# The levels of a block inverse on the half of the columns that each level changes

## The chip, the cores and the metric

The kernel runs on one core of a Trainium2 chip. The metric is the device time of one execution in microseconds (us), the median of several runs. TensorE is PE in the profile (PEld its weight loads), VectorE is DVE, ScalarE is ACT, GpSimd is POOL, SyncE is SP.

## The reference

Two transformer blocks run one after the other on 512 tokens of width 1024. The first has attention with rotary positions beside a convolution branch. The second mixes tokens with a recurrence (RWKV-7) of 12 heads of width 64, beside attention over a memory, and then has a feed-forward layer. All is fp32. The part that this case touches is the recurrence:

```python
def step(S, inp):
    r_t, w_t, k_t, v_t, a_t, b_t = inp
    sa = jnp.einsum('bhvk,bhk->bhv', S, a_t)
    S = (S * w_t[:, :, None, :] + sa[..., None] * b_t[:, :, None, :]
         + v_t[..., None] * k_t[:, :, None, :])
    return S, jnp.einsum('bhvk,bhk->bhv', S, r_t)
```

## The kernel before

The engines run five programs that are written out by hand and wait for one another by semaphores. There is no scheduler: the order of each engine is the order of its code. PSUM has eight banks; `psum_order` lists every product in the order in which PE makes it, with its bank.

The recurrence is done in chunks of C = 64 tokens, for NP = 6 pairs of heads. A pair has 2 heads x 8 chunks = 16 systems of 64 rows. The chunks are split by parity q over the two halves of the 128 partitions, so an operand of one head is `[rows(q), h, c, :]` with c in 0 to 3 and 64 columns. For each system the kernel needs X, the inverse of I - N, with N strictly triangular. X starts as the inverse of the 2x2 diagonal blocks and grows by levels b = 2, 4, 8, 16, 32: a level knows the diagonal blocks of size b and fills in those of size 2b. It keeps X twice, as `XN` and transposed as `XT`, side by side in `XX`. In the level loop of pair p, for both heads h:

- PE, `times_inverse` (L982): y = NT x XN, 8 matmuls for each head, each with a 64x64 stationary operand and 64 moving columns. The result is in PSUM as `y{b}_{p}_{h}`, 256 columns.
- DVE (L2026): Y = y times the mask `m{b}`, which leaves the off-diagonal blocks of the level; 128x256.
- PE, `inverse_update` (L992): two products for each system, Y with XT (L1000) and XT with Y (L1003), 16 matmuls for each head, one PSUM tensor of two banks. In the last level `last_update` (L1008, matmul in L1013) makes the first of the two alone.
- DVE (L2052): the products are added into X, in the half of the columns that the level changes: 128x256 out of both banks, 128x128 in the last level.

Each such fp32 matmul stands in the trace as two records of MATMUL and two of LDWEIGHTS: 8 matmuls for each of two heads are "x32".

Other work is written between these steps. On PE: in level 2 the mean of the group norm of pair p - 1 (`gn_mean`), in level 4 its squares and the value projection of pair p + 1 in two halves, in level 8 `masked_values` (L1026), in level 16 the gate and `bonus_sum`. On DVE: in level 2 `gn_centre` and `unit_key`, in level 4 `decayed_a`, in level 8 the input of the next v, `gn_finish` and a `weights_low` (L1663), in level 16 `decayed_b`, `gate` and `bonus`. In the last pair, p = 5, units of the memory attention (`memory_unit`) stand there. After the levels comes `solve` (L1036), which multiplies by XT with 128 moving columns. L955 are the transposes ahead of the levels, L977 products of keys before these, L714 the modulation products, with a stationary operand of 2 columns, L727 small transposes of 2 moving columns.

POOL does little: it clears `GLU` (L629), waits until the norm of the second block's input is summed, clears the first state `H` (L631), and then makes one product for each pair (L641).

Of the kernel before, what the change touches and what calls it, by code (L numbers as in the profile page):

```python
# [63 lines left out]
G = 4  # L64
# [254 lines left out]
def build(nc, small, tables, xT, ctxT, memT, weights, saved, outT):  # L319
    plan = psum_plan()  # L320
    with ExitStack() as ctx:
# [86 lines left out]
        at = half + 6 * S  # L408
        XX_AT = at
        XX = region(at, 2, S); at += 2 * S  # L410
        NT, Y, TK, TV, MAK, MRK = (region(at + i * S, NC, C) for i in range(6)); at += 6 * S
        GT, RP, FB = (region(at + i * S, NC, C) for i in range(3)); at += 3 * S

        def heads_first(x):
            return x.rearrange("p (h c) t -> p h c t", h=HEADS)
# [5 lines left out]
        NT, Y, MAK, MRK = map(heads_first, (NT, Y, MAK, MRK))  # L421
        TK, TV = map(pairs_first, (TK, TV))

        inputs = 10 * S
# [41 lines left out]

        def rows(half):
            return slice(half * DH, (half + 1) * DH)

        def by_head(name):  # L470

# [59 lines left out]
        def bank_on(name):  # L531

            return psum[:, plan[name][0] * S:8 * S]

        def is_full(name):

# [108 lines left out]
        def _(pe):  # L645
# [345 lines left out]

            def inverse_update(name, h):  # L992

                take(name)
                out = bank(name).rearrange("p (k c t) -> p k c t", k=2, t=C)
# [12 lines left out]
            def last_update(name, h):  # L1008

                out = take(name, G * C).rearrange("p (c t) -> p c t", c=G)  # L1010
                for c in range(G):
                    for q in range(PARITIES):
                        ins = pe.matmul(out[rows(q), c, :], Y[rows(q), h, c, :], XT[rows(q), h, c, :],  # L1013
                                        start=True, stop=True)
                        if c == G - 1:
                            full_inc(ins, name)

# [74 lines left out]
            for p in range(NP):  # L1092
# [14 lines left out]
                for b in LEVELS:  # L1107
                    for h in range(HEADS):
                        if prev is None:
                            pe.wait_ge(x_first, p + 1)  # L1110
                        else:
                            pe.wait_ge(*is_free(f"x{prev}_{p}_{h}"))
                        times_inverse(f"y{b}_{p}_{h}", h)

                    if p and b == LEVELS[0]:
                        gn_mean(p - 1)
# [12 lines left out]
                    for h in range(HEADS):  # L1129

                        pe.wait_ge(*is_free(f"y{b}_{p}_{h}"))
                        if b != LEVELS[-1]:
                            inverse_update(f"x{b}_{p}_{h}", h)
                        else:

                            last_update(f"xf_{p}_{h}", h)
# [442 lines left out]
        def _(vec):  # L1579
# [426 lines left out]
            for p in range(NP):  # L2006
# [15 lines left out]
                for b in LEVELS:  # L2022
                    for h in range(HEADS):
                        name = f"y{b}_{p}_{h}"
                        vec.wait_ge(*is_full(name))
                        free_inc(vec.tensor_tensor(Y[:, h], bank(name, G * C).rearrange("p (c t) -> p c t", c=G),  # L2026
                                                   mask(f"m{b}", G), ALU.mult), name)

                    if p and b == LEVELS[0]:
                        gn_centre(p - 1)  # L2030
# [8 lines left out]
                    for h in range(HEADS):  # L2039

                        if b != LEVELS[-1]:
                            name = f"x{b}_{p}_{h}"
                            vec.wait_ge(*is_full(name))
                            new, old = (y[:, at:at + 2 * (S - b)].rearrange("p (k n) -> p k n", k=2)[:, :, 0:G * C]
                                        .rearrange("p k (n two b) -> p k n two b", two=2, b=b)[:, :, :, 0, :]
                                        for y, at in ((bank_on(name), b), (work, XX_AT + h * G * C + b)))
                        else:
                            name = f"xf_{p}_{h}"
                            vec.wait_ge(*is_full(name))
                            new, old = (y.rearrange("p (n two b) -> p n two b", two=2, b=b)[:, :, 1, :]  # L2050
                                        for y in (bank(name, G * C), XX[:, 0, h * G * C:(h + 1) * G * C]))
# [256 lines left out]
```

## Time and profile before

| | us |
|---|---|
| median of 3 runs | 1251.21 (1249.71 to 1251.71) |
| the profiled execution, device time | 1245.89 |
| its span, first to last instruction | 1243.8 |
| PE busy | 1124.5 (90%) |
| DVE busy | 648.4 (52%) |
| ACT busy | 458.1 (37%) |
| the level stages of pairs 0 to 5 | from about 480 to 805 |

Span and busy times come from one profiled execution. Its device time is 5.3 us below the median of the runs. The busy time of an engine is summed over the span, where the stages have different limits. [...]

### The profile page before, as it was taken

To read this page: it belongs to the slowest core of one execution; us is meant where nothing else is said; L and a number is where in the kernel's file an instruction comes from. 1 tells how busy PE (TensorE), PEld (TensorE's weight loads), DVE (VectorE), ACT (ScalarE), POOL (GpSimd) and SP (SyncE) were. 2 spreads that over 40 slices of the span, in tenths; PEclk is the share of its full clock that TensorE was granted. 3 is DMA by queue.
4 is the path that set the end of the run, shared out by engine and by line. 5 is a ranking of instruction groups with operands and counts; after the bars stand their busy time and mean duration, and the time that the engine had idled before them with its cause. 6 is when DMAs were issued, how large, how long until landed. Compare 5 with 4: busy or idle time off the path is not lost.

```text
span 1243.8 us, 21886 instructions
## 1 busy us (share of the span) xinstructions
PE 1124.5 (90%) x9476; PEld 837.2 (67%) x9476; DVE 648.4 (52%) x1057; ACT 458.1 (37%) x736; POOL 9.9 (1%) x12
## 2 busy tenths in 40 slices
PE   6999999677799787888888898899799999999998
PEld 4377776344468566666666665668588888888887
DVE  2478777886544666464655643674633323233332
ACT  3233353346642453323232322352445311345211
POOL 0000000000000000000000000000000000000000
PEclk9999999799899898989899999999899999999999
DMA  8832223200022211101010003103233333323330
GB/s 320 294 121 66 85 85 114 73 1 1 1 71 82 74 62 38 38 32 36 19 36 19 19 3 121 52 26 101 61 92 94 102 102 88 99 85 102 102 110 26
DMA packets 25582, 94.93 MB, mean 76 GB/s; under 512 B 2833, under 2 KB 2833, under 8 KB 24977
## 3 DMA queue, kind: packets, MB, share of 16 engines
q1 hardware_dynamic: 25488, 93.54, 23.3%
q8 instruction: 76, 1.25, 0.4%
q14 instruction: 18, 0.14, 0.0%
HBM read 89.34 MB, written 4.19 MB: 75 GB/s over the span
## 4 chain that ended last, share of the span: by engine, by line
PE 50%; DVE 9%; ACT 2%; issue 2%; ACTq 0%; DVEq 0%
PE psum L689 13%; PE psum L690 13%; PE psum L691 13%; PE psum L699 3%; PE psum L987 2%; PE psum L1000 1%; PE psum L1036 1%; DVE pair_weights_low L1663 1%; DVE work L2052 1%; PE psum L955 1%; PE psum L1003 1%; PE psum L1079 1%; DVE work L2014 1%; PE psum L1059 1%; PE psum L1013 1%
## 5 line engine op out<-in xcount | busy, mean ns | idle before, releaser
L1663 DVE TENSOR_TENSOR weights_low<-ring,weights_high 128x1024 fp32r<-128x1024 f32 x72 | 88.2, 1225 | 82.8 <-ACT weights_high L1334 82.8
L1334 ACT ACTIVATE weights_high<-ring 128x1024 fp32r<-128x1024 f32 x72 | 75.9, 1054 | 127.7 <-PE psum L691 127.7
L689 PE MATMUL psum<-normed_high,weights_high 128*128 128x512 f32 x256 | 102.7, 401 | 4.8 <-DVE normed_low L1668 4.2
L690 PE MATMUL psum<-normed_low,weights_high 128*128 128x512 f32 x256 | 102.1, 399 | 0.0
L691 PE MATMUL psum<-normed_high,weights_low 128*128 128x512 f32 x256 | 101.9, 398 | 0.0
L689 PE MATMUL psum<-hidden_high,weights_high 128*128 128x512 f32 x256 | 99.6, 389 | 0.0
L690 PE MATMUL psum<-hidden_low,weights_high 128*128 128x512 f32 x256 | 99.6, 389 | 0.0
L691 PE MATMUL psum<-hidden_high,weights_low 128*128 128x512 f32 x256 | 99.6, 389 | 0.0
L1284 ACT ACTIVATE work<-psum 128x384 f32<-128x384 f32 (+2 forms) x124 | 59.6, 510 | 96.1 <-PE psum L1036 51.0
L689 PE MATMUL psum<-pair_normed_high,pair_weights_high 128*128 128x512 f32 x176 | 76.6, 435 | 12.3 <-DVE normed_low L1668 4.3
L2141 DVE TENSOR_TENSOR hidden_low<-work,hidden_high 128x512 fp32r<-128x512 f32 x32 | 22.2, 693 | 110.3 <-ACT hidden_high L1573 110.3
L1592 DVE SCALAR_TENSOR_TENSOR work<-work,small_sb 128x512 f32<-128x512 f32 x116 | 79.2, 745 | 0.0
L689 PE MATMUL psum<-normed_high,in_weights_high 128*128 128x512 f32 x176 | 71.6, 407 | 1.6 <-DVE in_weights_low L1663 1.6
L691 PE MATMUL psum<-pair_normed_high,pair_weights_low 128*128 128x512 f32 x176 | 69.7, 396 | 0.0
L690 PE MATMUL psum<-normed_low,pair_weights_high 128*128 128x512 f32 x176 | 69.7, 396 | 0.0
L691 PE MATMUL psum<-normed_high,in_weights_low 128*128 128x512 f32 x176 | 69.6, 396 | 0.0
L690 PE MATMUL psum<-normed_low,in_weights_high 128*128 128x512 f32 x176 | 69.6, 395 | 0.0
L689 PEld LDWEIGHTS psum<-normed_high,weights_high 128*128 128x128 f32 x256 | 48.5, 189 | 19.4 <-issue 5.4
L691 PEld LDWEIGHTS psum<-normed_high,weights_low 128*128 128x128 f32 x256 | 48.7, 190 | 11.8
L690 PEld LDWEIGHTS psum<-normed_low,weights_high 128*128 128x128 f32 x256 | 48.7, 190 | 11.2
L689 PEld LDWEIGHTS psum<-hidden_high,weights_high 128*128 128x128 f32 x256 | 48.0, 188 | 10.1
L691 PEld LDWEIGHTS psum<-hidden_high,weights_low 128*128 128x128 f32 x256 | 48.0, 188 | 10.0
(235 smaller groups left out, 2115.2 us busy)
## 6 DMA issues: line engine op xcount, KB each, us to landing
ring<-weights SPq DMA_DIRECT2D x154, 512.0 KB, 3.6
residual<-xT SPq DMA_DIRECT2D x1, 2048.0 KB, 18.4
residual_saved<-residual SPq DMA_DIRECT2D x8, 256.0 KB, 2.0
residual<-residual_saved SPq DMA_DIRECT2D x1, 2048.0 KB, 8.7
outT<-residual SPq DMA_DIRECT2D x8, 256.0 KB, 3.2
work<-memT SPq DMA_DIRECT2D x1, 1024.0 KB, 5.0
work<-ctxT SPq DMA_DIRECT2D x1, 1024.0 KB, 9.7
small_sb<-small SPq DMA_DIRECT2D x1, 907.0 KB, 7.7
```

The costliest lines, as they stand in the source:

```text
L689: pe.matmul(out, wh, high(k), start=first and n == 0, stop=False)
L690: pe.matmul(out, wh, low(k), start=False, stop=False)
L691: ins = pe.matmul(out, wl, high(k), start=False, stop=last and n == len(order) - 1)
L699: full_inc(pe.matmul(take(name, w), stationary, moving, start=True, stop=True), name)
L955: last = pe.transpose(out[:, c, :], src[:, 2 * c:2 * c + 2, :], tab("ident"))
L987: ins = pe.matmul(out[rows(q), c, :], NT[rows(1 - q), h, c, :], XN[rows(1 - q), h, c, :], start=True, stop=True)
L1000: ins = pe.matmul(out[rows(q), 0, c, :], Y[rows(q), h, c, :], XT[rows(q), h, c, :], start=True, stop=True)
L1284: free_inc(act.activation(out, bank(name, w) if src is None else src, ACT.Copy), name)
L1334: act.activation(WH[group(q)][:, q % 2, :], ring[:, SLOT[b], :], ACT.Copy).then_inc(w_high, 1)
L1592: return vec.scalar_tensor_tensor(out=out, in0=a, scalar=scalar, in1=b, op0=op, op1=ALU.add)
L1663: vec.tensor_tensor(WL[group(q)][:, q % 2, :], ring[:, SLOT[b], :], WH[group(q)][:, q % 2, :].bitcast(F32), ALU.subtract).then_inc(w_low, 1)
L2141: vec.tensor_tensor(FL[:, t, :], FS[:, t, :], FH[:, t, :].bitcast(F32), ALU.subtract).then_inc(h_low, 1)
```

## The change

A level changes only the columns of its odd blocks of X (in the transposed copy; even blocks in the other), and Y is zero in half of its columns. The change moves only these columns through PE.

- `times_inverse` takes only the even blocks of XN as moving columns, 32 in place of 64, and writes 32 columns for each system. The mask reads 128x128 and writes into the even blocks of Y.
- The odd blocks of Y have to be zero, and the even blocks differ from level to level. So each level has a Y of its own, `Y[b]`, in a region `YS` of 5 x 512 words for each partition. POOL clears it once, after `H`, and the first mask of pair 0 waits for that.
- `inverse_update` and `last_update` take 32 columns in place of 64 as moving operand, out of XT (odd blocks) or Y (even blocks). The whole Y or XT is still the stationary operand, 64x64.
- The additions have the same shape. They now read whole, contiguous PSUM rows instead of every second block.
- The regions that follow NT in the work buffer move by one place.

```diff
+        YS = region(at, len(LEVELS), S)
...
+        def blocks_of(x, b, odd):
+
+            return x.rearrange("p (n two b) -> p n two b", two=2, b=b)[:, :, odd, :]
...
             pool.memset(H[:, 0, :], 0.0).then_inc(zeroed, 1)
+            pool.memset(YS, 0.0).then_inc(zeroed, 1)
...
-            def times_inverse(name, h):
+            HALF = C // 2
...
-                out = take(name, G * C).rearrange("p (c t) -> p c t", c=G)
+            def times_inverse(name, h, b):
+
+                out = take(name, G * HALF).rearrange("p (c t) -> p c t", c=G)
                 for c in range(G):
                     for q in range(PARITIES):
-                        ins = pe.matmul(out[rows(q), c, :], NT[rows(1 - q), h, c, :], XN[rows(1 - q), h, c, :],
-                                        start=True, stop=True)
+                        ins = pe.matmul(out[rows(q), c, :], NT[rows(1 - q), h, c, :],
+                                        blocks_of(XN[rows(1 - q), h, c, :], b, 0), start=True, stop=True)
...
-                                ins = pe.matmul(out[rows(q), 0, c, :], Y[rows(q), h, c, :], XT[rows(q), h, c, :],
-                                                start=True, stop=True)
+                                ins = pe.matmul(out[rows(q), 0, c, :], Y[b][rows(q), h, c, :],
+                                                blocks_of(XT[rows(q), h, c, :], b, 1), start=True, stop=True)
                             else:
-                                ins = pe.matmul(out[rows(1 - q), 1, c, :], XT[rows(q), h, c, :], Y[rows(q), h, c, :],
-                                                start=True, stop=True)
+                                ins = pe.matmul(out[rows(1 - q), 1, c, :], XT[rows(q), h, c, :],
+                                                blocks_of(Y[b][rows(q), h, c, :], b, 0), start=True, stop=True)
...
                         vec.wait_ge(*is_full(name))
-                        free_inc(vec.tensor_tensor(Y[:, h], bank(name, G * C).rearrange("p (c t) -> p c t", c=G),
-                                                   mask(f"m{b}", G), ALU.mult), name)
+                        new = bank(name, G * C // 2).rearrange("p (c n b) -> p c n b", c=G, b=b)
+                        kept = Y[b][:, h].rearrange("p c (n two b) -> p c n two b", two=2, b=b)[:, :, :, 0, :]
+                        m = blocks_of(tab(f"m{b}"), b, 0)[:, None].to_broadcast([P, G, C // (2 * b), b])
+                        if (p, b, h) == (0, LEVELS[0], 0):
+                            vec.wait_ge(zeroed, 3)
+                        free_inc(vec.tensor_tensor(kept, new, m, ALU.mult), name)
...
-                            new, old = (y[:, at:at + 2 * (S - b)].rearrange("p (k n) -> p k n", k=2)[:, :, 0:G * C]
-                                        .rearrange("p k (n two b) -> p k n two b", two=2, b=b)[:, :, :, 0, :]
-                                        for y, at in ((bank_on(name), b), (work, XX_AT + h * G * C + b)))
+                            new = bank(name).rearrange("p (k n) -> p k n", k=2)[:, :, 0:G * C // 2].rearrange(
+                                "p k (n b) -> p k n b", b=b)
+                            at = XX_AT + h * G * C + b
+                            old = work[:, at:at + 2 * (S - b)].rearrange("p (k n) -> p k n", k=2)[:, :, 0:G * C].rearrange(
+                                "p k (n two b) -> p k n two b", two=2, b=b)[:, :, :, 0, :]
```

No instruction changes its place. What PE issues in level 2 of pair 0 was this (times_inverse for both heads, then the first matmuls of inverse_update; the last figures are partitions x moving columns, and a matmul counts once here):

```order
L987 MATMUL psum<-work 64x64 x16
L1000 MATMUL psum<-work 64x64
L1003 MATMUL psum<-work 64x64
L1000 MATMUL psum<-work 64x64
L1003 MATMUL psum<-work 64x64
```

and in the changed kernel it is this:

```order
L992 MATMUL psum<-work 64x32 x16
L1005 MATMUL psum<-work 64x32
L1008 MATMUL psum<-work 64x32
L1005 MATMUL psum<-work 64x32
L1008 MATMUL psum<-work 64x32
```

The number of matmuls and their order stay; only the moving columns are halved. On DVE, levels 16 and 32 of pair 1 were (masks, `decayed_b`, additions, `gate`, `bonus`, masks, last additions):

```order
L2026 TENSOR_TENSOR work<-psum,tables_sb 128x256 x2
L1957 TENSOR_TENSOR work<-work 128x512
L1961 TENSOR_TENSOR work<-work 128x512
L2052 TENSOR_TENSOR work<-psum,work 128x2x8x16 x2
L1978 TENSOR_TENSOR mixed<-psum,mixed 128x512
L1935 TENSOR_TENSOR work<-psum,work 128x512
L2026 TENSOR_TENSOR work<-psum,tables_sb 128x256 x2
L2052 TENSOR_TENSOR work<-psum,work 128x4x32 x2
```

and in the changed kernel they are:

```order
L2036 TENSOR_TENSOR work<-psum,tables_sb 128x8x16 x2
L1962 TENSOR_TENSOR work<-work 128x512
L1966 TENSOR_TENSOR work<-work 128x512
L2063 TENSOR_TENSOR work<-psum,work 128x2x8x16 x2
L1983 TENSOR_TENSOR mixed<-psum,mixed 128x512
L1940 TENSOR_TENSOR work<-psum,work 128x512
L2036 TENSOR_TENSOR work<-psum,tables_sb 128x4x32 x2
L2063 TENSOR_TENSOR work<-psum,work 128x4x32 x2
```

The masks have half of their elements, in runs of b; nothing else differs.

## Rows read from the trace of the kernel before

**Rows 1.** The head of the page.
```profile
span 1243.8 us, 21886 instructions
...
PE 1124.5 (90%) x9476; PEld 837.2 (67%) x9476; DVE 648.4 (52%) x1057; ACT 458.1 (37%) x736; POOL 9.9 (1%) x12
```

**Rows 2.** Windows over the level stages of pairs 1 and 4.
```profile
core 0: us, PE busy (x) PEld busy (x) DVE busy (x) ACT busy (x) POOL busy (x), PEclk, DMA share, GB/s
536.20:560.70 24.50, 21.91 (x515) 16.82 (x516) 14.96 (x31) 4.71 (x8) 0.00 (x0) 1.00 0.08 24
716.30:742.60 26.30, 23.70 (x515) 17.82 (x515) 14.94 (x31) 4.69 (x7) 0.00 (x0) 0.92 0.01 2
```

**Rows 3.** The chain that ended last, pair 1, levels 16 and 32: start, us, what.
```profile
555.09 0.67 DVE work L2026 x2
...
557.00 0.75 DVE work L2052 x2
...
558.94 0.34 DVE work L2026
...
559.32 1.15 PE psum L1013 x32
```

**Rows 4.** Timeline of DVE, pair 2, levels 2, 4 and 8.
```profile
598.83 0.69 DVE L1592 SCALAR_TENSOR_TENSOR mixed<-psum,mixed 128x512 f32<-128x512 f32 x1 [0.59 <-PE psum L699]
...
605.87 0.42 DVE L2052 TENSOR_TENSOR work<-psum,work 128x256 f32<-128x256 f32 x1 [3.49 <-PE psum L1003]
...
611.99 0.89 DVE L2052 TENSOR_TENSOR work<-psum,work 128x256 f32<-128x256 f32 x2 [0.23 <-PE psum L1000]
```

**Rows 5.** Groups by line and form: masks and additions.
```profile
L2026 DVE TENSOR_TENSOR work<-psum,tables_sb 128x256 f32<-128x256 f32 x60 | 23.8, 419 | 11.4 <-PE psum L987 11.1
L2052 DVE TENSOR_TENSOR work<-psum,work 128x256 f32<-128x256 f32 x48 | 19.8, 422 | 37.3 <-PE psum L1003 33.7 <-PE psum L1000 2.7
L2052 DVE TENSOR_TENSOR work<-psum,work 128x128 f32<-128x128 f32 x12 | 3.5, 292 | 3.8 <-PE psum L1013 3.8
```

**Rows 6.** Timeline of PE: runs of records of one line.
```profile
600.13 1.15 PE L987 MATMUL psum<-work 64*64 64x64 f32 x32 [0.25 <-DVE work L2052]
...
621.00 1.96 PE L1036 MATMUL psum<-work 64*64 64x128 f32 x32 [0.16 <-issue]
...
57.60 0.62 PE L727 MATMUL psum<-tables_sb,work 2*128 2x2 f32 x8
```

**Rows 7.** By line: durations in ns, minimum/median/maximum, first and last start.
```profile
L714 PEld LDWEIGHTS psum<-ring,small_temps x48: 80/85/85, 28.1 to 219.8; 128*2 128x2 f32 x48
...
L987 PEld LDWEIGHTS psum<-work x960: 129/135/228, 480.6 to 800.9; 64*64 64x64 f32 x192
L987 PE MATMUL psum<-work x960: 218/218/366, 480.6 to 800.9; 64*64 64x64 f32 x192
...
L699 PEld LDWEIGHTS psum<-head_squares,tables_sb x44: 186/188/338, 25.5 to 828.0; 128*128 128x128 f32 x44
...
L1036 PE MATMUL psum<-work x192: 269/269/321, 501.3 to 807.0; 64*64 64x128 f32 x192
...
L727 PEld LDWEIGHTS psum<-tables_sb,work x8: 133/136/138, 57.6 to 58.0; 2*128 2x128 f32 x8
L727 PE MATMUL psum<-tables_sb,work x8: 190/196/197, 57.6 to 58.0; 2*128 2x2 f32 x8
```

**Rows 8.** Timeline of POOL.
```profile
0.73 1.91 POOL L629 MEMSET work<- 128x2168 f32 x1 [0.29 <-POOLq L2300]
```

**Rows 9.** Windows at the low clock, and the product of keys ahead of pair 3.
```profile
529.30:536.00 6.70, 5.48 (x47) 4.71 (x48) 6.28 (x10) 2.83 (x5) 0.85 (x1) 0.50 0.05 22
590.70:597.40 6.70, 5.38 (x44) 4.65 (x46) 4.71 (x8) 2.39 (x4) 0.00 (x0) 0.50 0.00 0
710.20:720.30 10.10, 8.46 (x66) 5.71 (x62) 6.17 (x10) 2.84 (x5) 0.00 (x0) 0.50 0.01 2
...
649.26 1.98 PE L977 MATMUL psum<-work 64*64 64x128 f32 x32 [2.65 <-DVE head_rstd L1927]
```

More of the change, by code:

```diff
@@ L410, in build @@
         XX = region(at, 2, S); at += 2 * S
-        NT, Y, TK, TV, MAK, MRK = (region(at + i * S, NC, C) for i in range(6)); at += 6 * S
+        NT, TK, TV, MAK, MRK = (region(at + i * S, NC, C) for i in range(5)); at += 5 * S
         GT, RP, FB = (region(at + i * S, NC, C) for i in range(3)); at += 3 * S
+        YS = region(at, len(LEVELS), S)
         def heads_first(x):
@@ L420, in build @@
         XT, XN = (heads_first(XX[:, i, :].rearrange("p (n t) -> p n t", t=C)) for i in range(2))
-        NT, Y, MAK, MRK = map(heads_first, (NT, Y, MAK, MRK))
+        NT, MAK, MRK = map(heads_first, (NT, MAK, MRK))
+        Y = {b: heads_first(YS[:, i, :].rearrange("p (n t) -> p n t", t=C)) for i, b in enumerate(LEVELS)}
         TK, TV = map(pairs_first, (TK, TV))
@@ L529, in bank @@
             return psum[rows, b * S:b * S + (w or n * S)]
-        def bank_on(name):
-            return psum[:, plan[name][0] * S:8 * S]
         def is_full(name):
@@ L980, in key_products, with inverse_update @@
                             full_inc(ins, name)
-            def times_inverse(name, h):
-                out = take(name, G * C).rearrange("p (c t) -> p c t", c=G)
+            HALF = C // 2
+            def times_inverse(name, h, b):
+                out = take(name, G * HALF).rearrange("p (c t) -> p c t", c=G)
                 for c in range(G):
                     for q in range(PARITIES):
-                        ins = pe.matmul(out[rows(q), c, :], NT[rows(1 - q), h, c, :], XN[rows(1 - q), h, c, :],
-                                        start=True, stop=True)
+                        ins = pe.matmul(out[rows(q), c, :], NT[rows(1 - q), h, c, :],
+                                        blocks_of(XN[rows(1 - q), h, c, :], b, 0), start=True, stop=True)
                         if c == G - 1:
                             full_inc(ins, name)
-            def inverse_update(name, h):
+            def inverse_update(name, h, b):
                 take(name)
-                out = bank(name).rearrange("p (k c t) -> p k c t", k=2, t=C)
+                out = bank(name).rearrange("p (k c t) -> p k c t", k=2, t=HALF)
                 for c in range(G):
@@ L999, in inverse_update, with last_update @@
                             if k == 0:
-                                ins = pe.matmul(out[rows(q), 0, c, :], Y[rows(q), h, c, :], XT[rows(q), h, c, :],
-                                                start=True, stop=True)
-                            else:
-                                ins = pe.matmul(out[rows(1 - q), 1, c, :], XT[rows(q), h, c, :], Y[rows(q), h, c, :],
-                                                start=True, stop=True)
+                                ins = pe.matmul(out[rows(q), 0, c, :], Y[b][rows(q), h, c, :],
+                                                blocks_of(XT[rows(q), h, c, :], b, 1), start=True, stop=True)
+                            else:
+                                ins = pe.matmul(out[rows(1 - q), 1, c, :], XT[rows(q), h, c, :],
+                                                blocks_of(Y[b][rows(q), h, c, :], b, 0), start=True, stop=True)
                             if c == G - 1:
                                 full_inc(ins, name)
-            def last_update(name, h):
-                out = take(name, G * C).rearrange("p (c t) -> p c t", c=G)
+            def last_update(name, h, b):
+                out = take(name, G * HALF).rearrange("p (c t) -> p c t", c=G)
                 for c in range(G):
                     for q in range(PARITIES):
-                        ins = pe.matmul(out[rows(q), c, :], Y[rows(q), h, c, :], XT[rows(q), h, c, :],
-                                        start=True, stop=True)
+                        ins = pe.matmul(out[rows(q), c, :], Y[b][rows(q), h, c, :],
+                                        blocks_of(XT[rows(q), h, c, :], b, 1), start=True, stop=True)
                         if c == G - 1:
@@ L1112, in _ @@
                             pe.wait_ge(*is_free(f"x{prev}_{p}_{h}"))
-                        times_inverse(f"y{b}_{p}_{h}", h)
+                        times_inverse(f"y{b}_{p}_{h}", h, b)
                     if p and b == LEVELS[0]:
@@ L1132, in _ @@
                         if b != LEVELS[-1]:
-                            inverse_update(f"x{b}_{p}_{h}", h)
+                            inverse_update(f"x{b}_{p}_{h}", h, b)
                         else:
-                            last_update(f"xf_{p}_{h}", h)
+                            last_update(f"xf_{p}_{h}", h, b)
                         if p + 1 < NP and b == LEVELS[1] and h == 0:
@@ L2049, in _ @@
                             vec.wait_ge(*is_full(name))
-                            new, old = (y.rearrange("p (n two b) -> p n two b", two=2, b=b)[:, :, 1, :]
-                                        for y in (bank(name, G * C), XX[:, 0, h * G * C:(h + 1) * G * C]))
+                            new = bank(name, G * C // 2).rearrange("p (n b) -> p n b", b=b)
+                            old = blocks_of(XX[:, 0, h * G * C:(h + 1) * G * C], b, 1)
                         free_inc(vec.tensor_tensor(old, new, old, ALU.add), name)
```

## The prediction

> **What bounds the kernel now.** The page's head comes first: TensorE (PE) is busy 90% of a 1243.8 us span, and the VectorE (DVE) is busy 52% [rows 1]. That is an average. The change lies in the inversion stage of the six head pairs, so the next view is the table of windows over that stage: 24.5 us for pair 1 and 26.3 for pair 4, with PE busy 21.9 and 23.7 us of it [rows 2]. Outside of the six stages nothing is edited but one memset. PE's busy time counts the whole latency of overlapping small matmuls, so it does not say that PE sets the pace of the stage.
>
> Then the chain of waits, inside one stage (pair 1). From 555.09 us it runs on DVE: both masks of level 16 (0.67), then after `decayed_b` both additions of level 16 (0.75), the first mask of level 32 (0.34), and only then PE's last update [rows 3]. In the earlier levels (timeline of pair 2) it is different. In level 2 the centring of the last pair's output (598.83) stands between the masks and the additions. In level 4 the first addition waits 3.49 us for PE, which has half of the v projection ahead of each update. In level 8 the additions at 611.99 wait 0.23 us for PE [rows 4]. So a shorter mask pays in levels 16 and 32; elsewhere PE or other DVE work sets the time.
>
> **The mask (DVE).** It reads 128x256 out of PSUM in 419 ns; after the change it reads and writes 128x128. The nearest row is the last addition, 128x128 with PSUM in and strided out, 292 ns; the same line at 128x256 takes 422 [rows 5]. It is strided now already, in runs of 2 to 32 elements, and the by-form row gives one mean for all of them, so I price short runs at nothing. A mask saves 419 - 292 = 127 ns. There are 60. On the path:
> - Level 16, pairs 0 to 4: both masks, 2 x 127 = 254 ns, five times: 1.27 us.
> - Level 32, pairs 0 to 4: the first mask only, since the last update then runs through both heads without a gap (1.15 us for both, [rows 3]): 5 x 0.127 = 0.64 us.
> - Level 2 of pair 0, which has no earlier pair to centre: one mask, 0.13 us.
> - Pair 5: PE and the memory attention's units stand between mask and update; nothing.
> Sum 2.04 us. The other 44 masks or so are hidden, by PE's side products and by centring; that is 5.6 us of DVE time with no effect.
>
> **The matmuls (PE).** This is the disputed cost. Each matmul of the three helpers keeps its 64x64 stationary operand and its count, and moves 32 columns in place of 64. A fp32 matmul stands in the trace as two records, each with a weight load. What sets the gap from one record to the next in the same part of the array, the columns that stream or the load?
> - Streaming: with 128 columns (the solve, 32 records in two parts of the array, 1.96 us less its own 0.27 over 15.5 steps) the gap is 109 ns. With 64 columns it is (1.15 - 0.22)/16 = 58, more than the half of 109 [rows 6, 7].
> - Loading: the shortest load, of 2 columns, takes 85 ns, of 64 columns 135, of 128 columns 188 [rows 7]. That is about 50 ns for each 64 columns above a fixed part: a load of 64 columns needs 50 to 53 ns, as long as 64 columns stream.
> - A case where next to nothing streams: the transposes L727 move 2 columns behind a load that lasts 136 ns, as ours does. Eight take 0.62 us; less the 0.196 of the last that is 61 ns a step, not 10 [rows 6, 7].
> So at 32 columns I take the load as the bound and the gap as unchanged at 58. Bounds: from 58 - 27 = 31 ns (streaming alone, half of 53 gone) up to 61 (L727's). What does get shorter is the end of each group: the last record drains 32 columns sooner. 128 columns take 269 and 64 take 218, so 32 save 25 ns [rows 7]. Four or five such ends lie on the chain in each pair (y of level 2, second update of levels 4 and 8, last update): 6 x 4 x 0.025 = 0.6 us.
>
> [...]
>
> **The rest.** The additions keep shape and element count; PSUM is now read contiguously where it was strided: priced at nothing, bound by the 422 against 419 of a contiguous read [rows 5]. Reading the moving operand in runs of 2 or 4 has no row here; if it doubled the stream of 32 columns it would be back at 53 ns, behind the load. The memset of 2560 words a partition runs on POOL after that of `H`, at about 412 us. A memset of 2168 takes 1.91, so this one 2.3, done by 415. The first mask, which waits for it, comes after the first y product at 480.6 [rows 7, 8]. Cover 65 us. If it disturbed DVE, which is then on the path, it would cost at most its own 2.3; no row speaks for it. The separate buffers remove no wait: the masks wait only for their product.
>
> **Sum.** 2.04 + 0.6 = 2.6, so the profiled execution goes from a span of 1243.8 to 1241.2 and from its 1245.9 to 1243.3. The three runs have their median at 1251.2, 5.3 above that execution. 1251.2 - 2.6 = 1248.6.
>
> **The rivals.**
> 1. *The clock, and slower.* Each of pairs 0 to 4 enters the stage out of a stretch at granted clock 0.5 (1.2 GHz), around the place where PE has waited for DVE ahead of its key products (2.65 us in pair 3): 6.7 us before pairs 1 and 2, but 10.1 us around the start of pair 4 [rows 9]. Pair 4's stage takes 26.3 against 24.5 us [rows 2]: a stretch of that extra length costs 1.8 us. The change takes columns away just there, in the first products of the levels. If that lets the low clock last longer, one more such stretch leaves -0.8, two cancel the gain at +1.0, and all four pairs that lack it now give 4 x 1.8 - 2.6 = +4.6, 1255.8. For it: pair 2's low stretch reaches to 597.4, into its y product. Against: before pair 1 it ends before the stage starts at 536.2, and at 0.5 the transposes and products of other lines fill PE as before. It decides from two stretches on.
> 2. *Streaming sets the gap, and much faster.* With 31 in place of 58, a y group of both heads gets 0.43 us shorter, an update of one head 0.21. On the chain of a pair: y of level 2 (0.43), y of level 4 and its two updates (0.6), half of y and the update of level 8 (0.6), the last update (0.2): 1.85 a pair, 11 in six, with the 2.6 above 13.6: 1237.6. For it: the gap does follow columns from 128 to 64. Against: L727 and the load durations. An in-between gap of 45 gives half of the 11, and 1243.1.
> 3. *The masks do not get shorter* (short runs or the repeated mask cost what was saved): only the ends are left, 1250.6, no change. Against: the additions at 292 and 422.
>
> **How the numbers follow.** Load-bound with the clock as now: 0.60. Since its 2.6 us is 0.21% of the time, just at the bound, I give 0.36 of it to faster and 0.24 to same. Rival 2 or the in-between gap: 0.19, all faster. Rival 1: 0.16, half in same (one or two stretches), half slower. Rival 3: 0.05, same. So faster 0.55, same 0.37, slower 0.08. About 0.2% is what a measurement of this kernel tells from no change, which is 2.5 us. The range goes from 1243, the in-between gap, to 1253, two and a half extra stretches; it leaves out the full rival 2 and most of the slower part of rival 1.
>
> **What the profile after will show.** The masks at 128x128 and near 292 ns. If the load sets the gap, 32 records of y still last about 1.13 us, and matmul durations are near 193; if streaming does, they last near 0.7. The stage of pair 1 at 24.0 instead of 24.5. In the windows, the length of each stretch at 0.5: longer than 6.8 in more pairs than one means rival 1. The memset at 412 should last about 2.3 us, and the first mask of pair 0 should have no wait from POOL. I am wrong if the gap falls well under 58, or if the stages get shorter by more than 0.7 us with the masks at 292.

## The result, and the profile after

The changed kernel takes 1273.38 us (median of 4 runs, 1265.43 to 1278.82). The kernel before takes 1251.46 beside it (4 runs, 1249.71 to 1252.88). The ratio is 1.0164, with a 95% interval of 1.0126 to 1.0202: slower. The forecast was 1248.6, with a range up to 1253. A ratio here is not the quotient of the two medians. The ratios further down count every run, except that of the changed kernel with ten idle matmuls, which leaves out the five of its ten runs that lie over 1.5% above the fastest.

The head of the page of the changed kernel, with the granted clock in 40 slices:

```profile
span 1274.2 us, 21888 instructions
...
PE 1156.1 (91%) x9476; PEld 862.0 (68%) x9476; DVE 641.3 (50%) x1057; ACT 458.1 (36%) x736; POOL 12.1 (1%) x13
...
PEclk9999999799999988888887979989899999999999
```

Beside [rows 1], PE has the same 9476 matmuls with fewer columns to move, and yet it is busy for 31.6 us more (1156.1 against 1124.5). DVE is busy 7.1 us less. PE did the same operations on less data and was busy for longer, so it ran slower. The clock row says so (the granted clock is the share of full speed that TensorE was given in a stretch; 1.00 is all of it): of the twelve slices over the levels (the 16th to the 27th) nine show 8 or 7, where the page of the kernel before has three. The mean granted clock of the profiled execution is 0.939; before it was 0.968.

The windows over the six level stages of the changed kernel, each from its first y product to its first product of `solve`:

```profile
core 0: us, PE busy (x) PEld busy (x) DVE busy (x) ACT busy (x) POOL busy (x), PEclk, DMA share, GB/s
480.80:503.40 22.60, 21.67 (x510) 18.39 (x508) 11.37 (x27) 2.75 (x5) 0.00 (x0) 0.85 0.09 26
538.50:567.10 28.60, 26.58 (x514) 20.27 (x514) 13.86 (x31) 4.60 (x7) 0.00 (x0) 0.80 0.08 21
604.20:632.40 28.20, 26.33 (x514) 20.22 (x514) 13.61 (x31) 4.57 (x7) 0.00 (x0) 0.80 0.08 21
668.90:698.40 29.50, 27.13 (x514) 20.81 (x514) 13.58 (x30) 4.56 (x7) 0.00 (x0) 0.79 0.07 20
736.60:765.20 28.60, 26.66 (x514) 20.24 (x514) 13.87 (x31) 4.56 (x7) 0.00 (x0) 0.80 0.01 2
799.40:834.00 34.60, 31.85 (x546) 21.93 (x544) 18.38 (x62) 10.39 (x33) 0.00 (x0) 0.84 0.18 69
sum 172.10, PE 160.22 PEld 121.85 DVE 84.66 ACT 31.42 POOL 0.00; mean PE 26.70 PEld 20.31 DVE 14.11 ACT 5.24 POOL 0.00
```

The sum is 172.1. The same six windows of the kernel before give 20.6, 24.4, 25.1, 24.7, 26.2 and 30.1, together 151.1; [rows 2] has two of them. So the stages have 21.0 of the 30.4 us by which the span grew. Another 7.5 lie between the stages (from `solve` to the next y product: 181.1 against 173.6) and 1.8 after the last one. No stage of the changed kernel has a clock of 1.00; of the kernel before, pair 4 (0.92) and pair 2 (0.97) alone were under it.

The windows over the long stretches at the low clock, a granted clock of 0.50, changed kernel:

```profile
532.80:549.80 17.00, 15.36 (x154) 11.54 (x155) 8.59 (x16) 4.24 (x7) 0.00 (x0) 0.50 0.01 2
597.60:614.70 17.10, 15.77 (x176) 11.72 (x169) 9.46 (x18) 4.79 (x9) 0.15 (x1) 0.50 0.01 2
662.50:679.50 17.00, 15.59 (x171) 11.51 (x164) 9.26 (x17) 4.71 (x8) 0.00 (x0) 0.50 0.01 2
730.70:747.80 17.10, 15.30 (x154) 11.47 (x155) 8.75 (x17) 4.26 (x8) 0.00 (x0) 0.50 0.01 2
822.90:836.60 13.70, 13.70 (x114) 10.29 (x116) 4.18 (x16) 3.12 (x10) 0.00 (x0) 0.51 0.01 1
```

In [rows 9] such a stretch lasted 6.7 us ahead of pairs 1 and 2 and ended about where the levels began; at pair 4 it lasted 10.1. Now it begins near the same place, within about 1 us of the end of PE's wait ahead of the key products, but in pairs 1 to 4 it lasts 17.0 and reaches over level 2 into level 4. Pair 0 has a second stretch of 6.8 us inside its levels, and in pair 5 there is a new one, in the last levels. Added up over the records of the granted clock, the low clock inside the six stages went from 5.6 to 64.6 us. For 59.0 us more of it the stages got 21.0 us longer: 0.36 us for each. PE's busy row doesn't give this away, since 15.36 of 17.00 us is 90% busy. Where the recorded texts write 1.2 and 2.4 GHz, the traces show the shares 0.50 and 1.00; no run shows the frequencies.

The timeline of PE shows where the clock comes back in pair 1:

```profile
543.96 1.92 PE L992 MATMUL psum<-work 64*64 64x32 f32 x32
...
548.53 0.63 PE L694 MATMUL psum<-pair_normed_high,pair_weights_low 128*128 128x512 f32 x1
...
549.99 0.40 PE L692 MATMUL psum<-pair_normed_high,pair_weights_high 128*128 128x512 f32 x1
```

What PE did before it rose was level 2, the y product of level 4, the squares of the group norm and then the v projection, which moves 512 columns with each matmul. Its matmuls came 0.43 us apart at 0.50 and come 0.23 us apart at 1.00. A y product of both heads took 1.92 us at the low clock. At the full clock it takes 1.12, in the same kernel:

```profile
624.18 1.12 PE L992 MATMUL psum<-work 64*64 64x32 f32 x32 [0.26 <-DVE work L2063]
```

The groups by line and form, and the durations by line, of the changed kernel:

```profile
L2036 DVE TENSOR_TENSOR work<-psum,tables_sb 128x128 f32<-128x128 f32 x60 | 16.3, 288 | 18.5 <-PE psum L992 18.4
L2063 DVE TENSOR_TENSOR work<-psum,work 128x256 f32<-128x256 f32 x48 | 19.9, 423 | 50.5 <-PE psum L1008 46.9 <-PE psum L1005 3.2
...
L992 PE MATMUL psum<-work x960: 186/219/313, 480.6 to 826.1; 64*64 64x32 f32 x192
```

The masks take 288 ns, the additions are unchanged [rows 5]. But DVE's waits ahead of the additions grew from 37.3 to 50.5 us, and those ahead of the masks from 11.4 to 18.5. A y record lasts 219 ns at full clock, as long as with 64 columns (218 [rows 7]), and 291 at the low clock; the 186 is a single record.

### The profile page after: what moved, and what is told of

Read it like the earlier page. It is cut to its first block, busy times and chain, and to the rows that moved or that the text cites. A ratio compares the mean times of both kernels' runs of the same rounds, so it can differ in the third digit from the quotient of the medians.

```text
span 1274.2 us, 21888 instructions
## 1 busy us (share of the span) xinstructions
PE 1156.1 (91%) x9476; PEld 862.0 (68%) x9476; DVE 641.3 (50%) x1057; ACT 458.1 (36%) x736; POOL 12.1 (1%) x13
## 4 chain that ended last, share of the span: by engine, by line
PE 52%; DVE 8%; ACT 2%; issue 2%; ACTq 0%
PE psum L692 13%; PE psum L693 12%; PE psum L694 12%; PE psum L702 3%; PE psum L992 2%; PE psum L1041 1%; PE psum L1005 1%; PE psum L958 1%; DVE pair_weights_low L1668 1%; PE psum L1018 1%; PE psum L1084 1%; PE psum L1008 1%; PE psum L910 1%; PE psum L1064 1%; DVE work L2063 1%
## 5 line engine op out<-in xcount | busy, mean ns | idle before, releaser
L692 PE MATMUL psum<-pair_normed_high,pair_weights_high 128*128 128x512 f32 x176 | 80.3, 456 | 12.3 <-DVE normed_low L1673 4.3
L692 PEld LDWEIGHTS psum<-pair_normed_high,pair_weights_high 128*128 128x128 f32 x176 | 34.9, 198 | 31.8 <-issue 11.0
## 6 DMA issues: line engine op xcount, KB each, us to landing
residual<-xT SPq DMA_DIRECT2D x1, 2048.0 KB, 18.5
```

The costliest lines, as they stand in the source:

```text
L692: pe.matmul(out, wh, high(k), start=first and n == 0, stop=False)
```

## The experiments

The theory after the result (theory A in the expectations): with the gap set by the load, PE moves half of the columns in the same time. With that, TensorE is held at a granted clock of 0.50 for longer, into the levels. Its rivals were another cost of the narrow products themselves (operands read in runs of 2 to 32), and a cost of the masks, the separate buffers or the memset. Each expectation stands as it was written ahead of the run. The ratio is always to the kernel before, run on the same chip.

### Masks, buffers and memset alone

All matmuls move 64 columns again. What is left is the short mask, `Y[b]` and the memset. Against the changed kernel:

```diff
-                                        blocks_of(XN[rows(1 - q), h, c, :], b, 0), start=True, stop=True)
+                                        XN[rows(1 - q), h, c, :], start=True, stop=True)
...
-                        new = bank(name, G * C // 2).rearrange("p (c n b) -> p c n b", c=G, b=b)
+                        new = bank(name, G * C).rearrange("p (c n two b) -> p c n two b", c=G, two=2, b=b)[:, :, :, 0, :]
```

and the same in `inverse_update`, `last_update` and the additions.

> Y of each level in its own buffer, cleared once, and masks of 128x128, but every matmul moves all its 64 columns as in the kernel before. Theory A (the time was lost because fewer moving columns keep the clock at 1.2 GHz for longer): the low stretches are those of the kernel before (about 0.967 mean clock, 6.8 us ahead of each pair), and the shorter masks leave their 2 us: 1249.3, ratio 0.998. Theory B (the buffers, the memset or the masks in short runs cost the time): 1265 or more.

Measured: 1247.66 us (12 runs), ratio 0.9977 (0.9951 to 1.0003). None of the loss is in this part. The interval includes 1, so the runs alone don't show the 2 us of the masks. The stretches were not quite those of the kernel before: in the profiled execution those of pairs 1 to 4 last 10.2 us and end inside the stage, as here in pair 2, and of the low clock 16.1 us fall into the stages, where the kernel before has 5.6 and the changed one 64.6:

```profile
596.40:622.20 25.80, 23.53 (x517) 17.69 (x515) 13.86 (x31) 4.39 (x7) 0.00 (x0) 0.93 0.07 23
```

### The y products alone, and the updates alone

Two kernels take the changed one apart by function. The first moves 32 columns in `times_inverse` only (960 of the 2688 records), the second in `inverse_update` and `last_update` only (1728). Both keep the short masks.

> As the changed kernel, but only the first product of each level moves 32 columns; the updates move 64. Theory A: part of the loss. The y products are 960 of the 2688 narrow records, so by their share 7 to 8 of the 22 us: 1259, with the low stretch longer in some pairs. If the stretch depends on what runs just at the start of a stage, where y of level 2 stands, it is most of the loss, 1265 to 1273. Theory B: as the changed kernel, 1273.

Measured: 1257.75 us (8 runs), ratio 1.0062 (1.0029 to 1.0096).

> As the changed kernel, but only the updates move 32 columns; y moves 64. Theory A: 1728 of the 2688 records, so by share 14 of the 22 us: 1265; less if the start of the stage decides. Theory B: 1273.

Measured: 1251.49 us (10 runs), ratio 0.9999 (0.9970 to 1.0028). Windows over pairs 1 and 2 of the kernel with narrow y products, one line each:

```profile
543.50:567.40 23.90, 21.63 (x514) 16.68 (x514) 13.73 (x31) 4.64 (x7) 0.00 (x0) 0.99 0.09 25
604.20:632.60 28.40, 26.54 (x514) 20.26 (x516) 13.54 (x30) 4.63 (x7) 0.00 (x0) 0.80 0.07 21
```

and over pair 1 of the one with narrow updates:

```profile
537.90:561.90 24.00, 21.72 (x516) 16.79 (x516) 13.89 (x31) 4.71 (x8) 0.00 (x0) 1.00 0.08 25
```

The same program gives a stage of 23.9 us at 0.99 and one of 28.4 at 0.80, within one execution. So what is lost goes with the clock, not with the instructions. The parts don't add up: by the ratios, narrow y products cost (1.0062 - 0.9977) x 1251 = 11 us over the masks alone, narrow updates 3, which is not clear of noise, and both, in the changed kernel, 23. The first expectation, 1259 by the share of the records, was met. The second, 1265, was missed: the updates are 1728 of the 2688 records and alone cost next to nothing.

### Thirty-two columns, moved twice

Every level product moves its 32 columns twice, so that 64 stream again. They are read in the same short runs as in the changed kernel, and the second half of each output is never read.

```diff
+        def again(x):
+
+            return x[:, None].to_broadcast([DH, 2, x.shape[1], x.shape[2]])
...
-                                        blocks_of(XN[rows(1 - q), h, c, :], b, 0), start=True, stop=True)
+                                        again(blocks_of(XN[rows(1 - q), h, c, :], b, 0)), start=True, stop=True)
```

> The changed kernel, with each matmul moving its 32 columns twice in a row (64 columns in strided runs, the second copy goes to unused PSUM), nothing reads the copy. Theory A: the gap between records stays 58 ns since the load takes that long anyway, the clock is that of the kernel before, and the time is 1249, the 22 us are gone although PE does more. Theory C (strided reads of the moving operand or the narrower PSUM rows are what slows PE): 1273 or slower. If streaming set the gap, this kernel would be slower than the changed one with records of y lasting 1.15 us in place of less; the trace of the changed kernel speaks against that already.

Measured: 1248.55 us (10 runs), ratio 0.9979 (0.9952 to 1.0006). Its y records by line, and its window over pair 1:

```profile
L996 PE MATMUL psum<-work x960: 213/218/367, 484.2 to 808.3; 64*64 64x64 f32 x192
...
539.90:565.60 25.70, 23.52 (x514) 17.68 (x515) 13.70 (x31) 4.68 (x7) 0.00 (x0) 0.93 0.08 23
```

More work, and some 25 us less than the changed kernel. That rules out the rival of the short runs: they are all here. The useless columns are what brings time and clock back to those of the masks alone (25.8 us and 0.93 for such a stage there).

### Idle matmuls ahead of the levels

Ten fp32 matmuls of 128x128, from constant tables into an unused part of PSUM, stand between the first key products and the wait for the second. PE waited there [rows 9], and there the low stretches began.

```diff
+            def keep_busy(p, n):
+
+                order_names = psum_order()
+                at = [x[0] for x in order_names].index(f"nf_{p}")
+                last = [x[0] for x in order_names[:at] if plan[x[0]][0] <= 7 < plan[x[0]][0] + plan[x[0]][1]][-1]
+                pe.wait_ge(*is_free(last))
+                for _ in range(n):
+                    pe.matmul(psum[:, 7 * S:7 * S + P], tab("ident"), tab("ones"), start=True, stop=True)
...
                 key_products(f"na_{p}", p, B[p % 2])
+                keep_busy(p, 10)
                 pe.wait_ge(kd_ready, p + 1)
```

They went into three kernels: the changed one, the masks alone, and the kernel before.

> The changed kernel, and in each pair ten idle-time matmuls of 128x128 fp32 (identity times ones into a free PSUM bank that nobody reads) between the products na and ka, where PE waits 2.6 us for DVE. They change no wait of any other engine. Theory A says that the 22 us are the clock and nothing else: the stretch at 1.2 GHz ahead of each stage goes away or gets shorter, and of the 22 us at least 10 come back, 1262 or less. If other things slow the changed kernel, its time stays at 1273 or grows by the matmuls, 2 us a pair if they do not fit the gap.

Measured: median 1261.01 us (10 runs). Five of them took 1244.9 to 1252.4 at a clock of 0.966 to 0.972, and five 1269.7 to 1276.1 at 0.944 to 0.953. The ratio of 0.9969 (0.9935 to 1.0002) is that of the first five. The median lies between two groups and is the time of no run: half of the runs lost nothing against the kernel before, the other half as much as the changed kernel.

> The kernel with short masks and full-width matmuls, and the same ten matmuls in each pair's gap. If idle PE ahead of ka is what sends the clock down, the five stretches of 6.8 to 10.3 us at 1.2 GHz disappear; at 0.4 us of time for each us at the low clock (31 us of span for 75 us more of it, from before to the changed kernel) the 48 us of this version are worth 15 to 19 us: 1230 to 1235. If the clock falls there for another reason, 1248, or up to 1258 with the matmuls on the path.

Measured: 1245.27 us (10 runs), ratio 0.9948 (0.9920 to 0.9975).

> The kernel before with the ten idle-time matmuls in each pair's gap and nothing else; it tells what the low stretch ahead of the stages costs there, and so how I should have priced my first rival. I priced a stretch of about 7 us ahead of the stage at nothing and its extension into the stage at 1.8 us. If a us at 1.2 GHz costs 0.4 us wherever it lies, five stretches less are 34 x 0.4 = 13 us: 1238. If only a low clock inside the stage costs, since ahead of it PE waits for DVE anyway (the short-mask version gained 2 to 3 us from the same matmuls), the time is 1247 to 1250.

Measured: 1247.98 us (12 runs), ratio 0.9971 (0.9944 to 0.9998). Windows over pairs 2 and 5 of the changed kernel with idle matmuls (its profiled execution is one of the five at the higher clock; none of the other five was profiled):

```profile
593.90:617.70 23.80, 21.65 (x515) 16.82 (x513) 13.85 (x31) 4.59 (x8) 0.00 (x0) 1.00 0.08 24
768.30:802.60 34.30, 31.55 (x544) 21.79 (x542) 18.35 (x62) 10.49 (x33) 0.00 (x0) 0.85 0.16 65
```

over pairs 2 and 5 of the masks with idle matmuls:

```profile
595.60:619.60 24.00, 21.93 (x515) 16.81 (x515) 13.78 (x31) 4.69 (x8) 0.00 (x0) 1.00 0.07 24
770.60:805.20 34.60, 31.87 (x547) 22.02 (x546) 18.21 (x62) 10.14 (x31) 0.00 (x0) 0.85 0.17 67
```

and over pair 3 of the kernel before with idle matmuls:

```profile
657.40:681.80 24.40, 21.81 (x516) 16.75 (x516) 15.08 (x31) 4.67 (x8) 0.00 (x0) 1.00 0.08 25
```

The three at a clock of 1.00 are the stages at full clock: 24.4 before, 24.0 with the short masks, 23.8 with the half columns too. The gains of the change exist and are as small as the forecast had them; the clock is what covers them. The second expectation was too hopeful with its 1230 to 1235. Of the third, the second case came out: 1247 to 1250, a low clock ahead of the stage cost next to nothing (1247.98 against 1250.31 beside it).

The idle matmuls remove all stretches ahead of pairs 1 to 4 of the masks, yet the ratio falls by 0.0029 only, 3.6 us, and the two intervals overlap. The two profiled executions of the masks, without and with idle matmuls, show two reasons. Between the stages the low clock goes from 24.9 to 3.4 us, but the time only from 173.9 to 172.3: 0.07 us for each. There PE waits for DVE anyway, as the transposes ahead of the levels of pair 3 show, in the kernel before and then in the masks with idle matmuls:

```profile
651.74 1.97 PE L955 MATMUL psum<-tables_sb,work 128*128 128x128 f32 x8 [0.49 <-DVE work L2010]
654.20 1.70 PE L955 MATMUL psum<-tables_sb,work 128*128 128x128 f32 x8 [0.49 <-DVE work L2015]
```

```profile
650.21 1.09 PE L958 MATMUL psum<-tables_sb,work 128*128 128x128 f32 x8 [1.38 <-DVE work L2025]
652.67 1.09 PE L958 MATMUL psum<-tables_sb,work 128*128 128x128 f32 x8 [1.36 <-DVE work L2030]
```

At the low clock they take 1.97 us after a wait of 0.49, at the full clock 1.09 after a wait of 1.4; the second group starts 2.46 us behind the first either way. And inside the stages the idle matmuls gain 7.5 us in pairs 1 to 4, but pair 5 takes 34.6 us where it took 30.0, with 10.2 us at the low clock and none before. The same stands in the changed kernel with idle matmuls (34.3) and in the kernel before with them (33.0 against 30.1). So the low clock cost time where PE set the pace, as in pair 5 (4.6 us longer for 10.2 us of it), and 0.07 us for each us where PE waited. The masks with idle matmuls beat the kernel before by 0.5%.

### Half of the levels

The half columns in levels 2 and 4 only, then in levels 8, 16 and 32 only, with all masks short.

```diff
+                narrow = b <= 4
...
-                                        blocks_of(XN[rows(1 - q), h, c, :], b, 0), start=True, stop=True)
+                                        blocks_of(x, b, 0) if narrow else x, start=True, stop=True)
```

> The changed kernel with 32 moving columns in levels 2 and 4 only; levels 8, 16 and 32 move 64. In the trace of the changed kernel the low stretch reaches from ahead of the stage through levels 2 and 4 (17.1 us in pairs 1 to 4). Theory A, start of the stage decides: most of the loss, 1262 to 1273. By share of the records (1152 of 2688): 1258.

Measured: 1265.56 us (10 runs, 1251.5 to 1269.9), ratio 1.0073 (1.0030 to 1.0116).

> The changed kernel with 32 moving columns in levels 8, 16 and 32 only. Theory A, start of the stage decides: only the second, short stretches (3.4 us in each pair, around level 16) come, at 1.4 us each: 1250 to 1256. By share of the records (1536 of 2688): 1262.

Measured: 1260.62 us (10 runs), ratio 1.0079 (1.0044 to 1.0114). Windows over pair 1 with levels 2 and 4 narrow, then over pairs 1 and 5 with levels 8 to 32 narrow:

```profile
542.40:571.20 28.80, 26.80 (x515) 20.27 (x515) 13.88 (x31) 4.61 (x7) 0.00 (x0) 0.80 0.07 20
```

```profile
539.10:565.20 26.10, 23.96 (x510) 18.08 (x509) 13.53 (x30) 4.88 (x8) 0.00 (x0) 0.89 0.08 23
...
787.20:825.00 37.80, 35.06 (x548) 23.61 (x546) 18.78 (x63) 10.63 (x33) 0.00 (x0) 0.75 0.18 70
```

There are two places, one for each set of levels. Narrow early levels prolong the stretch that PE brings along from its wait, in pairs 1 to 4, and add one in pair 0 (pair 5 takes 29.9 us in that kernel, as before). Narrow late levels send the clock down anew within pair 5, where the memory attention's units stand between the products: 19.4 of the 32.1 us of low clock in the stages lie there.

That the start of the stage decides was borne out in half. The first median lies in its range of 1262 to 1273, with four of the ten runs below it. The second expectation, 1250 to 1256, was missed; 1260.62 is near the 1262 by share. Over the masks alone the early levels cost 12 us by the ratios and the late ones 13. Cut by level, the parts do add up to about the 23 of the whole.

### More idle matmuls

Four and three more, ahead of the transposes `ta` and `tk`, in the changed kernel and in the one with the masks alone.

> The changed kernel with more idle-time matmuls ahead of each stage: ten between na and ka as before, four ahead of the first transposes and three ahead of the third, where PE waits 1.4 us each time for DVE in the version with ten. With ten alone the changed kernel fell into two groups of runs, 1245 to 1252 at a clock of 0.966 to 0.972 and 1270 to 1276 at 0.944 to 0.953. Theory A (a stage that starts at 2.4 GHz stays there, one that starts low falls behind): the slow group becomes rare, median 1243 to 1250. If the narrow matmuls of the stage itself send the clock down, the slow group stays and the median is above 1255.

Measured: 1264.83 us (4 runs), ratio 1.0130 (1.0085 to 1.0174).

> Short masks, full-width matmuls and the seventeen idle-time matmuls of a pair. Ten gave 1245.3 against 1251.6. The low stretches that are left there lie outside pairs 1 to 4, so the other seven should change little: 1243 to 1246; slower than 1246 if they delay the transposes.

Measured: 1249.16 us (12 runs), ratio 0.9986 (0.9962 to 1.0010). Pair 5 of the changed kernel with 17 idle matmuls:

```profile
782.90:820.30 37.40, 34.66 (x546) 23.47 (x546) 18.34 (x62) 10.43 (x33) 0.00 (x0) 0.75 0.10 38
```

Of the first expectation, theory A's 1243 to 1250 failed, and the other case came out: a median above 1255, if the narrow matmuls of the stage itself send the clock down. Pairs 1 to 4 are repaired (23.8 to 24.5 us), but pair 5 is not: the fall lies inside its levels, behind the idle matmuls. The seven extra matmuls bought the masks nothing, and the second expectation, 1243 to 1246, was missed too. The clock is not the reason: its mean over the runs is 0.976, with ten it was 0.974. In the profiled executions the stages are 4.1 us shorter with seventeen (146.6 against 150.7), but the time ahead of the first stage and between the stages is 6.6 us longer. Which of the extra matmuls cost that stays open; the two were not run on the same chip.

### What sets the gap

Twelve matmuls (24 records) in the wait of each pair of the kernel with short masks, with other sizes in each pair: stationary by moving columns (64, 64) twice, (64, 32), (64, 8), (32, 32), (32, 64).

> The disputed cost by itself: the kernel with short masks and full-width matmuls, with twelve fp32 matmuls (24 records) in each pair's gap ahead of ka, in one quarter of the array, of a stationary operand of 64 rows by w columns and m moving columns: (w, m) = (64, 64) in pairs 0 and 1, (64, 32) in pair 2, (64, 8) in pair 3, (32, 32) in pair 4, (32, 64) in pair 5. If the load sets the gap: 58 ns in the first three kinds at 2.4 GHz, about 32 for (32, 32), and 56 to 58 for (32, 64). If streaming does: 58, 31, 10 to 25, 31, 58.

Measured: 1252.19 us (one run). Its timeline of PE has one row for each run of 24 records. "64*32" is rows by columns of the stationary operand, and the second size ends with the moving columns:

```profile
531.97 1.56 PE L969 MATMUL psum<-tables_sb 64*64 64x64 f32 x24
...
592.74 1.53 PE L969 MATMUL psum<-tables_sb 64*64 64x32 f32 x24
...
650.97 1.51 PE L969 MATMUL psum<-tables_sb 64*64 64x8 f32 x24
...
709.97 0.94 PE L969 MATMUL psum<-tables_sb 64*32 64x32 f32 x24
...
773.60 1.52 PE L969 MATMUL psum<-tables_sb 64*32 64x64 f32 x24
```

Less the last record's own duration (218, 219, 199, 193 and 216 ns in the order of the rows) and over 23 steps, the gap with 64 stationary columns is 58 ns with 64 moving columns and 57 with 32 and with 8: (1.51 - 0.20)/23 for the last. It is (0.94 - 0.19)/23 = 33 with 32 by 32, and 57 again when 64 columns stream over 32. In these five rows the gap goes with the larger of the two counts, so the longer of load and stream set it. That is the forecast's reading, now shown. For 8 columns the expectation had 10 to 25 ns if streaming set the gap; measured is 57. All 24 records of a row lie in one quarter of the array and come one at a time. The 32 records of a y product, spread over two parts, took 1.15 us [rows 6], where 32 such steps would take 1.8: the two parts ran side by side.

## Why the prediction was wrong

- *The masks*: 292 ns forecast, 288 measured. The stage at full clock went from 24.4 to 24.0 with them, as forecast. Right.
- *The load sets the gap* and half of the columns leaves it at 58 ns: right, within 2 ns. The y product of both heads was to last about 1.13 us and lasts 1.12, (1.12 - 0.22)/16 = 56 ns a step. The rival with the stream as the bound is out, by the table of gaps. One of the forecast's three readings for it was no test: the load of L727 is 128 columns wide ([rows 7], "2*128"), twice ours. It lasts as long as ours (136 ns), but with 50 ns for each 64 columns its gap would be about 100, not 61. The experiment with 8 moving columns is the test.
- *The ends of groups*, 25 ns each: right in size, but not for the reason given. The records were to last about 193 ns, and at full clock they last 219. A y product is 30 ns shorter (1.12 against 1.15) because its 16 steps take 56 ns in place of 58. The stage at full clock is 23.8 against 24.0.
- *The memset* of `YS` was to last 2.3 us and cost nothing. It lasts 2.23 and ends 67 us ahead of the first mask, which waits for PE alone:

```profile
412.07 2.23 POOL L634 MEMSET work<- 128x2560 f32 x1
...
481.29 0.29 DVE L2036 TENSOR_TENSOR work<-psum,tables_sb 128x128 f32<-128x128 f32 x1 [0.61 <-PE psum L992]
```

- **The step that failed is rival 1, the clock**: its "Against: ... at 0.5 the transposes and products of other lines fill PE as before", the price of 1.8 us for an extra stretch, with at most four of them, and so the chance of 0.16. That fewer columns in the first products of the levels could let the low clock last longer was named, and the sign given for it, stretches longer than 6.8 us in more pairs than one, came true: 17.0 to 17.1 us in four. But it was taken to happen in a stage or not, at the price that pair 4 showed, where 4.0 us of the low clock fell into the stage. In fact the stretches of pairs 1 to 3 went from 6.8 to 17 us and that of pair 4 from 10.1, with 11.1 to 12.5 us inside each of the stages of pairs 1 to 4, 6.8 in pair 0, and 11.0 in pair 5, for which no stretch was reckoned at all. At the measured 0.36 us each, 59 us more of the low clock cost 21, where the rival's worst case was 7.2.
- The step behind it: from a gap that doesn't change the forecast went on to a PE that works as before, but for the ends of groups. What changes is how much streams in each gap. The forecast priced what the smaller matmuls take and not what they do to the clock.

The chain of cause is shown as follows. Take the half columns away, and the loss goes (masks alone). Let the same columns stream twice, and it goes too, with the strided reads kept. Keep the half columns and hold the clock with other work ahead of the levels, and the stages of pairs 1 to 4 fall to 23.8, the shortest measured; but this held in five of ten runs only, and not in pair 5. Over the 144 runs of the first eight experiments and of the kernel before beside them, a straight line of the time against the time at the low clock (2 x (1 - mean clock) x time) has a slope of 0.37 us per us, a correlation of 0.95, and leaves 2.4 us of scatter. That agrees with the 0.36 of the stages.

Open is why the parts by function add up to less than the whole: 11 and 3 us against 23. The clock in the records is 0.50 or 1.00, never between, and with narrow y products alone pairs 1 and 2 of one execution had means of 0.99 and 0.80 over the same products; where it turns was not measured. Open too is why the same kernel with ten idle matmuls falls into two groups of runs, and why pair 5 loses its clock behind them.

## What to carry to other kernels

Before you make matmuls narrower, look for what sets their gap. Here it was the load, 57 to 58 ns with 8, 32 or 64 moving columns, and little was gained: 0.6 us a stage at full clock, from the shorter masks and from steps of 56 in place of 58 ns. Then look at the granted clock of the stretches ahead of and inside the stage. Here the stages of pairs 1 to 4 were entered at 0.50, out of a wait of PE (2.65 us in pair 3 [rows 9]), and took 28.2 to 29.5 us, where such a stage took 23.8 at full clock in the version with idle matmuls. In this kernel the low clock cost 0.36 us per us inside the stages, where PE set the pace, and 0.07 between them, where PE waited for DVE.

## What was not expected of the hardware

- The same number of records at nearly the same gap (56 against 58 ns at full clock), with half of the moving columns, came with a mean granted clock of 0.939, where it was 0.968.
- The gap that the load sets grew with the low clock. At 0.50 the narrow y product takes 1.92 us against 1.12, so that (1.92 - 0.29)/16 = 102 ns is its gap, where it is 56 at the full clock. With 64 columns a y product at the low clock takes 1.97 us, a gap of (1.97 - 0.31)/16 = 104, so half of the columns didn't protect from it. Pair 4 of the kernel before:

```profile
716.31 1.97 PE L987 MATMUL psum<-work 64*64 64x64 f32 x32
```

- Ten idle matmuls for each pair, in a wait of 2.65 us [rows 9], raised the clock of the kernel before from 0.968 to 0.975 in the profiled executions, and its time fell by 0.3% (0.9944 to 0.9998). The timeline of PE of the masks with idle matmuls, pair 3:

```profile
645.01 2.50 PE L968 MATMUL psum<-tables_sb 128*128 128x128 f32 x20
```
